# The expert pass of a two-block network: fixed order of experts, weights in a ring of slots, split products

## The reference, cut to what matters

```python
g_top = top_1(t @ rg_w + rg_b)                # 1 of 4 groups
e_top = top_2(t @ re_w[g] + re_b[g])          # 2 of its 4 experts
for e in range(16):
    hid = silu(t @ w_gate[e]) * (t @ w_up[e])             # 1024 -> 512
    out = out + combine[:, e:e+1] * (hid @ w_down[e])     # 512 -> 1024
return rms_norm_2(h + out, final_norm_g)
```

## Time and profile before

| | us |
|---|---|
| median of 3 runs | 2615.15 (2611.01 to 2625.91) |
| the profiled execution, its own time | 2606.21 |
| its span | 2604.4 |
| TensorE busy (PE), share of the span | 2364.2, 91% |
| VectorE busy (DVE), share | 1160.2, 45% |
| ScalarE busy (ACT), share | 587.6, 23% |
| GpSimd busy (POOL), share | 731.7, 28% |
| mean granted TensorE clock | 0.95 |

### The profile page before, as it was taken

How to read it: one execution, slowest core, us unless ns; L and a number is a source line. 1 busy time by engine, 2 the same in 40 slices (tenths; PEclk the granted TensorE clock), 3 DMA queues, 4 the chain that set the end, 5 groups by cost and what they waited for, 6 DMA issues and landing times.

```text
span 2604.4 us, 28182 instructions
## 1 busy us (share of the span) xinstructions
PE 2364.2 (91%) x10934; PEld 1736.5 (67%) x10934; DVE 1160.2 (45%) x1501; ACT 587.6 (23%) x851; POOL 731.7 (28%) x420
## 2 busy tenths in 40 slices
PE   6899988899999999898998999998996885999994
PEld 3576637688888888664556888886875673444442
DVE  2488963364444443336645646542228422111113
ACT  2311113311111111325633111122334120110111
POOL 2100002533333334434335444444430331000001
PEclk8999987899999999999998999998999986999997
DMA  8445241262122221210012333232320224888885
GB/s 267 158 161 162 97 162 41 73 227 65 58 63 64 64 65 57 71 41 9 1 31 79 95 96 97 89 115 67 97 81 1 80 57 142 309 315 324 315 321 186
DMA packets 242054, 312.67 MB, mean 120 GB/s; under 512 B 13499, under 2 KB 199468, under 8 KB 235828
## 3 DMA queue, kind: packets, MB, share of 16 engines
q1 hardware_dynamic: 230140, 275.23, 32.4%
q0 software_dynamic: 7040, 25.72, 2.6%
q10 hardware_dynamic: 4791, 10.58, 1.1%
HBM read 286.31 MB, written 25.19 MB: 120 GB/s over the span
## 4 chain that ended last, share of the span: by engine, by line
PE 78%; issue 8%; DVE 6%; POOL 4%; DMA 3%; ACT 1%; DVEq 0%; POOLq 0%; ACTq 0%
PE acc L475 49%; PE acc L2151 9%; PE pb L2166 4%; PE pb L1827 2%; PE pa L1779 2%; PE acc L1953 2%; PE pa L1967 2%; PE pb L1980 2%; DMA mod_raw<-in_w_mod 2%; POOL wlo L458 1%; PE acc L522 1%; POOL y L601 1%; DVE hid_hi L1321 1%; PE acc L536 1%; PE pa L629 1%
## 5 line engine op out<-in xcount | busy, mean ns | idle before, releaser
L458 POOL TENSOR_TENSOR wlo<-raw,whi 128x1024 fp32r<-128x1024 f32 x204 | 509.2, 2496 | 969.1 <-ACT whi L447 969.0
L475 PE MATMUL acc<-ah,whi 128*128 128x256 f32 (+1 forms) x1616 | 514.7, 367 | 58.6 <-DVE al L641 36.2
L475 PE MATMUL acc<-al,whi 128*128 128x256 f32 (+1 forms) x1616 | 506.7, 362 | 0.0
L475 PE MATMUL acc<-ah,wlo 128*128 128x256 f32 (+1 forms) x1616 | 505.8, 362 | 0.0
L447 ACT ACTIVATE whi<-raw 128x1024 fp32r<-128x1024 f32 x218 | 230.3, 1059 | 1057.6 <-PE acc L475 1038.8
L475 PEld LDWEIGHTS acc<-ah,whi 128*128 128x128 f32 x1616 | 306.6, 191 | 120.6 <-issue 42.4
L475 PEld LDWEIGHTS acc<-al,whi 128*128 128x128 f32 x1616 | 309.8, 192 | 47.0 <-issue 0.5
L475 PEld LDWEIGHTS acc<-ah,wlo 128*128 128x128 f32 x1616 | 308.9, 191 | 46.9
L1330 DVE SCALAR_TENSOR_TENSOR x<-acc,mod,x 128x256 f32<-128x256 f32 (+1 forms) x192 | 121.1, 658 | 262.1 <-PE acc L475 262.0
L475 PE MATMUL acc<-hid_hi,whi 128*128 128x512 f32 (+1 forms) x768 | 230.8, 355 | 0.7 <-DVE x L1330 0.2
L475 PE MATMUL acc<-hid_lo,whi 128*128 128x512 f32 (+1 forms) x768 | 229.6, 353 | 0.0
(11 more groups left out here) (310 smaller groups left out, 2487.9 us busy)
## 6 DMA issues: line engine op xcount, KB each, us to landing
raw<-in_w_ff SPq DMA_DIRECT2D x128, 512.0 KB, 3.9
mod_raw<-in_w_mod SPq DMA_DIRECT2D x96, 512.0 KB, 5.3
wg<-in_expert_w_gate SPq DMA_DIRECT2D x16, 2048.0 KB, 8.6
wu<-in_expert_w_up SPq DMA_DIRECT2D x16, 2048.0 KB, 8.7
wd<-in_expert_w_down SPq DMA_DIRECT2D x16, 2048.0 KB, 10.0
raw<-in_w_in SPq DMA_DIRECT2D x30, 512.0 KB, 3.9
raw<-in_conv_w_pw SPq DMA_DIRECT2D x24, 512.0 KB, 7.2
expert_rows_dram<-zero_rows POOLq DMA_DIRECT2D x1, 12288.0 KB, 38.2
```

What stands on the lines that cost most here:

```text
L458: e.eng.tensor_tensor(wlo[b][:, :], raw[e.n["g"] % RING][:, :], whi[b][:, :].bitcast(F32), ALU.subtract).then_inc(S["lo_ready"], 1)
L475: ins = e.eng.matmul(o, w, m, start=keys.index(key) == n, stop=len(keys) - 1 - keys[::-1].index(key) == n)
```

## The change

The 48 KB in which wg, wu and wd lay become a ring of 12 slots of 1,024 values a partition (4 gate, 4 up, 4 down), loaded in pairs of 1 MB. ScalarE writes the high part of a slot into one of five buffers; VectorE writes the low part over the slot itself. The ten slots of gate, up and the first two of down are split so and multiplied in three fp32r terms; the last two of down stay f32. The rows and half of the hidden values are split too. The down product of a block is done one pass late, after the next block's gate and up products.

The list of blocks now begins with every expert once, in order, and further blocks of experts with more than 128 rows come behind. So the first two blocks need no routing result: the loads of the first expert's 12 slots are issued before the last projection is done, and the code of blocks 0 and 1 stands ahead of the loop, which runs over the rest (`more`, 14 here). A counter `weights_used` numbers the slots as TensorE uses them; all waits of SyncE, ScalarE and VectorE for free space are values of it. `count_of(i, each, more)` is i x each + more for the pair i = (loop variable, offset). One semaphore per pair of slots tells that its load has landed (before: one each for wg, wu and wd). The old loops are taken out (their lines are left out below).

```diff
+E_SLOTS = 12
+SPLIT_DOWN = 2
+E_SPLITS = 8 + SPLIT_DOWN
+E_HIGHS = 5
...
-    wg = sb("wg", [P, KT, E_FF], at=ah_at)
-    wu = sb("wu", [P, KT, E_FF], at=ah_at + 16384)
-    wd = sb("wd", [P, 4, D], at=ah_at + 32768)
+    expert_pair = [sb(f"expert_pair{r}", [P, 2 * D], at=ah_at + 8192 * r) for r in range(E_SLOTS // 2)]
+    expert_in = [expert_pair[r // 2][:, r % 2 * D:r % 2 * D + D] for r in range(E_SLOTS)]
+    expert_lo = [sb(f"expert_lo{r}", [P, D], F32R, ah_at + 4096 * r) for r in range(E_SLOTS)]
+    expert_hi = [sb(f"expert_hi{b}", [P, D], F32R, e_at + 4096 * b) for b in range(E_HIGHS)]
...
-    xgt = sb("xgt", [P, KT, P], at=h_at + 20480)
+    xgt_hi = sb("xgt_hi", [P, KT, P], F32R, h_at + 20480)
+    xgt_lo = sb("xgt_lo", [P, KT, P], F32R, h_at + 43008)
...
+    hidT_hi = sb("hidT_hi", [P, 4, P], F32R, h_at + 28672)
+    hidT_lo = sb("hidT_lo", [P, 4, P], F32R, h_at + 47104)
...
+    def weights_done(i, s):
+        return s + 1 if i is FIRST else count_of(i, E_SLOTS, s - 3)
+    def split_number(i, s):
+        return s if i is FIRST else count_of(i, E_SPLITS, s - SPLIT_DOWN)
+    def high_buffer(i, s):
+        return expert_hi[(s if i is FIRST else 8 + s) % E_HIGHS]
+    def expert_load(e, ex, s):
+        if s < 8:
+            src = A["expert_w_gate_2" if s < 4 else "expert_w_up_2"][0, ex].rearrange("e (p k) n -> p (e k n)", k=KT)
+        else:
+            src = A["expert_w_down_2"][0, ex].rearrange("e (p k) n -> p (e k n)", k=4)
+        e.eng.dma_start(expert_pair[s // 2][:, :], src[:, s % 4 * D:s % 4 * D + 2 * D]
+                        ).then_inc(S[f"expert_in{s // 2}"], 16)
+    def expert_high(e, i, s, n):
+        e.eng.wait_ge(S[f"expert_in{s // 2}"], count_of(i, 16, 16 if s < 8 else 0))
+        if i is not FIRST or n >= E_HIGHS:
+            e.eng.wait_ge(S["weights_used"], weights_done(i, n - E_HIGHS))
+        e.eng.activation(high_buffer(i, n)[:, :], expert_in[s][:, :], ACT.Copy).then_inc(S["expert_hi"], 1)
+    def expert_low(e, i, s, n):
+        e.eng.wait_ge(S["expert_hi"], split_number(i, n) + 1)
+        e.eng.tensor_tensor(expert_lo[s][:, :], expert_in[s][:, :], high_buffer(i, n)[:, :].bitcast(F32), ALU.subtract
+                            ).then_inc(S["expert_lo"], 1)
...
+        sp.wait_ge(S["acc_ready"], U_TOTAL - KT)
+        for s in range(0, E_SLOTS, 2):
+            expert_load(e, slice(0, 1), s)
...
+        for s in range(0, 8, 2):
+            sp.wait_ge(S["weights_used"], s + 2)
+            expert_load(e, slice(1, 2), s)
         sp.wait_ge(S["meta_ready"], 1)
...
+        more = sp.value_load(meta[0:1, LIST:LIST + 1], min_val=N_EXP - 2, max_val=SLOTS_MAX - 2)
+        def expert_of(i):
+            return bass.ds(sp.value_load(meta[0:1, bass.ds(count_of(i, 1, 0), 1)], min_val=0, max_val=N_EXP - 1), 1)
+        def load_parts(i, parts):
+            ex = expert_of(i)
+            for s in parts:
+                sp.wait_ge(S["weights_used"], weights_done(next_to(i, -1 if s < 8 else 0), s + 1))
+                expert_load(e, ex, s)
+        with sp.Fori(0, more) as i:
+            load_parts((i, 2), range(0, 8, 2))
+            load_parts((i, 1), range(8, E_SLOTS, 2))
+        load_parts((more, 1), range(8, E_SLOTS, 2))
...
+        def rows_high(i):
+            act.wait_ge(S["xg_turned"], count_of(i, 1, 2))
+            act.activation(xgt_hi[:, :, :], pa[:, :].rearrange("p (k q) -> p k q", q=P), ACT.Copy
+                           ).then_inc(S["xgt_hi"], 1)
+        def silu(i):
+            act.wait_ge(S["weights_used"], weights_done(i, 3))
+            if i is not FIRST:
+                act.wait_ge(S["hidt_ready"], count_of(i, 1, 0))
+            act.activation(gate_s[:, :], acc[0][:, 0:E_FF], ACT.Silu).then_inc(S["silu_gate"], 1)
+        def out_half(i, last=3):
+            act.wait_ge(S["weights_used"], weights_done(next_to(i, 1), last))
+            act.wait_ge(S["yo_out"], count_of(i, 16, 16))
+            act.activation(yo[:, 0:512], pbk[:, 0:512], ACT.Copy).then_inc(S["yo_act"], 1)
+        def out_rows(i):
+            act.wait_ge(S["yo_act"], count_of(i, 1, 1))
+            act.wait_ge(S["yo_dve"], count_of(i, 1, 1))
+            act.dma_start(yo_d[bass.ds(count_of(i, P, 0), P), :], yo[:, :]).then_inc(S["yo_out"], 16)
+        def expert_first():
+            expert_high(e, FIRST, 0, 0)
+            rows_high(FIRST)
+            for s in range(1, 8):
+                expert_high(e, FIRST, s, s)
+            silu(FIRST)
+        def expert_pass(i, rows_out):
+            expert_high(e, i, 0, 0)
+            rows_high(i)
+            for s in range(1, 4):
+                expert_high(e, i, s, s)
+            if rows_out:
+                out_half(next_to(i, -2), 11)
+            for s in range(4, 6):
+                expert_high(e, i, s, s)
+            if rows_out:
+                out_rows(next_to(i, -2))
+            for s in range(6, 8):
+                expert_high(e, i, s, s)
+            silu(i)
+            for s in range(8, 8 + SPLIT_DOWN):
+                expert_high(e, i, s, s)
+        expert_first()
+        expert_pass((None, 1), False)
         act.wait_ge(S["meta_ready"], 1)
...
+        more = act.value_load(meta[0:1, LIST:LIST + 1], min_val=N_EXP - 2, max_val=SLOTS_MAX - 2)
+        with act.Fori(0, more) as i:
+            expert_pass((i, 2), True)
+        for n in range(SPLIT_DOWN):
+            expert_high(e, (more, 2), 8 + n, n)
+        out_half((more, 0), 11)
+        out_rows((more, 0))
+        out_half((more, 1))
+        out_rows((more, 1))
...
+        base, further = rt[:, 17, 0:16], rt[:, 17, 16:32]
+        e.step(TS(base, ramp[:, 0:16], float(P), 16.0 * P, ALU.mult, ALU.add))
+        e.step(TT(further, upto, nb, ALU.subtract))
+        e.step(TT(further, further, ramp[:, 0:16], ALU.subtract))
+        e.step(TS(further, further, float(P), -float(P), ALU.mult, ALU.add))
+        ranks = pbk[:, 512:576].rearrange("p (b n) -> p b n", b=4)
         where = rt[:, 18, 0:64].rearrange("p (b n) -> p b n", b=4)
-        e.step(TT(where, pbk[:, 512:576].rearrange("p (b n) -> p b n", b=4),
-                  base.unsqueeze(1).to_broadcast([P, 4, 16]), ALU.add))
+        beyond = rt[:, 22, 0:64].rearrange("p (b n) -> p b n", b=4)
+        e.step(TS(beyond, ranks, float(P), None, ALU.is_ge))
+        e.step(TT(beyond, beyond, further.unsqueeze(1).to_broadcast([P, 4, 16]), ALU.mult))
+        e.step(TT(where, ranks, base.unsqueeze(1).to_broadcast([P, 4, 16]), ALU.add))
+        e.step(TT(where, where, beyond, ALU.add))
...
+        def rows_low(i):
+            dve.wait_ge(S["xgt_hi"], count_of(i, 1, 1))
+            TT(xgt_lo[:, :, :], pa[:, :].rearrange("p (k q) -> p k q", q=P), xgt_hi[:, :, :].bitcast(F32), ALU.subtract
+               ).then_inc(S["xgt_ready"], 1)
+        def hidden(i):
+            dve.wait_ge(S["silu_gate"], count_of(i, 1, 1))
+            dve.wait_ge(S["weights_used"], weights_done(i, 7))
+            TT(hidt[:, :], gate_s[:, :], acc[0][:, 512:1024], ALU.mult).then_inc(S["hidt_ready"], 1)
+        def hidden_turned(i):
+            dve.wait_ge(S["hid_turned"], count_of(i, 1, 1))
+            turned = acc[1][:, 0:E_FF].rearrange("p (k q) -> p k q", q=P)
+            if SPLIT_DOWN < 4:
+                dve.tensor_copy(hidT[:, SPLIT_DOWN:, :], turned[:, SPLIT_DOWN:, :])
+            dve.tensor_copy(hidT_hi[:, 0:SPLIT_DOWN, :], turned[:, 0:SPLIT_DOWN, :]).then_inc(S["hidT_high"], 1)
+            dve.wait_ge(S["hidT_high"], count_of(i, 1, 1))
+            TT(hidT_lo[:, 0:SPLIT_DOWN, :], turned[:, 0:SPLIT_DOWN, :], hidT_hi[:, 0:SPLIT_DOWN, :].bitcast(F32),
+               ALU.subtract).then_inc(S["hidT_ready"], 1)
+        def out_half(i, last=3):
+            dve.wait_ge(S["weights_used"], weights_done(next_to(i, 1), last))
+            dve.wait_ge(S["yo_out"], count_of(i, 16, 16))
+            dve.tensor_copy(yo[:, 512:1024], pbk[:, 512:1024]).then_inc(S["yo_dve"], 1)
+        def expert_first():
+            expert_low(e, FIRST, 0, 0)
+            rows_low(FIRST)
+            for s in range(1, 8):
+                expert_low(e, FIRST, s, s)
+            hidden(FIRST)
+        def expert_pass(i, rows_out):
+            expert_low(e, i, 0, 0)
+            rows_low(i)
+            for s in range(1, 4):
+                expert_low(e, i, s, s)
+            if rows_out:
+                out_half(next_to(i, -2), 11)
+            hidden_turned(next_to(i, -1))
+            for s in range(4, 8 + SPLIT_DOWN):
+                expert_low(e, i, s, s)
+            hidden(i)
+        expert_first()
+        expert_pass((None, 1), False)
         dve.wait_ge(S["meta_ready"], 1)
...
+        more = dve.value_load(meta[0:1, LIST:LIST + 1], min_val=N_EXP - 2, max_val=SLOTS_MAX - 2)
+        with dve.Fori(0, more) as i:
+            expert_pass((i, 2), True)
+        for n in range(SPLIT_DOWN):
+            expert_low(e, (more, 2), 8 + n, n)
+        out_half((more, 0), 11)
+        hidden_turned((more, 1))
+        out_half((more, 1))
```

(115 more changed lines are left out.)

49 lines of the change are left out of this document (3 added, 46 removed).

## The result

| | before | changed |
|---|---|---|
| median, us | 2617.06 (4 runs) | 2553.28 (4 runs, 2548.43 to 2561.81) |
| profiled execution, us | 2606.21 | 2548.4 |
| its span, us | 2604.4 | 2546.7 |
| PE / DVE / ACT / POOL busy, share of the span | 91 / 45 / 23 / 28% | 91 / 53 / 29 / 29% |

The ratio is 0.976 (95% interval 0.972 to 0.980). A later comparison of the same two kernels gave 2554.45 against 2610.58, ratio 0.980 (0.977 to 0.982). The forecast was 2553.

What follows compares the result with a forecast made beforehand. TensorE's own instructions bound the pass: 1.2 + 19.0 + 15 x 18.93 + 7.8 = 312.0 us against 374.1, a gain of 62.1; from the median 2615.15 that gives 2553 us, 8-in-10 range 2538 to 2590.

Steps and rivals of the forecast that it cites:

- The period: TensorE's time per expert block: 60 three-term matmuls, four f32 matmuls and transposes, 18.93 us in place of 23.18.
- Hand-offs covered: Forming and copying hidden rows in each pass lies beside other TensorE work; uncovered it would cost 2.3 us again.
- VectorE and ScalarE: Added splitting work per expert pass, 16.1 us on VectorE and 14.1 on ScalarE, fits beside TensorE's 18.93 and costs nothing.
- Rivals 2 and 3: Expert pass: VectorE's low parts too late, 2578 us, chance 0.06; at 2.5 us per part, slower, 2722 us, chance 0.04.
- Rival 4: No change: TensorE's clock falls in the expert pass, 8.5 us at half clock eating the gain, 2617 us; chance 0.03.
- Transfers: Expert pass needs 388 GB/s; bounds were 20.2 us by busy share or 17.8 to 18.3 by fast stretches, the latter taken.
- The step trusted least: Expert stretch: transfers keep 388 GB/s for 280 us, though no stretch of the trace was longer than 8 us.
- rival 1: Transfers become the bound of the expert pass, 20.2 us each by busy share, 19 us more, 2572 us; chance 0.18.
- Routing: Ahead of the expert pass: more small and 64-column steps on the chain to the positions, +1.2 us.
- Start of block 0: First expert block: high and low rows made in series where one copy stood before, 1.1 us more.
- The scatter: Ahead of the expert pass: early loads might free the scatter of one or two us, left out of the sum.
- The exit: After the last pass: the last block's hidden copies and down product, 7.8 us, loads having about 14 us before use.

Runs made afterwards that it cites:

- e4: Changed kernel with every product in f32 and no high or low parts, ring and late down product kept: 2587.07 us, 0.990 of the kernel before.
- e5: Changed kernel with the down product in its own block's pass, behind the turn of the hidden rows: 2570.8 us, 0.983 of the kernel before.
- e2: Changed kernel with all four down slots in three terms and six high buffers: 2541.57 us, 0.973 of the kernel before.
- e7: Changed kernel with one more unused load of 1 MB in each looped pass: 2569.91 us, 0.981 of the kernel before.
- e8: Changed kernel with 0.5 MB more loaded in each looped pass: 2551.03 us, 0.978 of the kernel before.
- e6: Changed kernel with the first expert's 6 MB of weights issued behind the routing result: 2565.82 us, 0.981 of the kernel before.
- e1: Changed kernel with the last block's down weights loaded earlier, into the first four slots: 2544.22 us, 0.974 of the kernel before.
- e3: Changed kernel with e1's early last down weights and e2's fully split down product together: 2534.25 us, 0.971 of the kernel before.

## Why the prediction was right, and where not

The time was 2553.0 against 2553.28. The mechanism was right; that the number agrees so closely is luck, as the terms were less exact than that. By the profiled executions the gain is 57.8 us where 62.1 was given; the median of the second comparison gives 56.1, that of the first 63.8.

- **Bound.** TensorE's own instructions, before and after: right, shown by the chain and by TensorE busy 243.44 of 243.44 us.
- **The period.** 18.93 given, 18.73 measured. The three-term matmul was put at 0.2286 and takes 0.232 in the pass (11.14 / 48), 0.2 us a pass too low; the twelve transposes were put at 1.77 and take 1.36, 0.4 too high (eight in 0.89, four in 0.47; the 0.59 for four came from a row that stands behind a wait). Over 15 passes the sum was 2.7 us too high (283.95 against 281.2).
- **Hand-offs covered.** Right: e4 puts their price before at 1.2 us a pass, e5 at 2.0 if they were opened again now. Even the small waits for low parts that the prediction allowed for didn't come.
- **VectorE and ScalarE.** 16.1 and 14.1 us given, 15.3 and 12.4 measured in the window, which counts overlapping records once; the operations' means add up to 16.1 and 12.8. The low parts took 1.22, as given. The hidden copies 0.41 each against 0.42. ScalarE reloads no table in the loop, 1.28 us a pass less. Rivals 2 and 3 are out: the longest of the 160 low parts took 1.232 us, and at 96% (e2) VectorE still isn't waited for. Rival 4 is out too, with a granted clock of 1.00 over the 243 us.
- **Transfers.** The choice between the bounds was right and too careful: 402 to 412 taken, 422 sustained (e7). The step trusted least, 388 GB/s for 280 us, held with 390 over 243. The other bound, 20.2 us from the busy share, fails, and rival 1 with it: e8 moves 421 GB/s in passes of 18.73. By the Trainium skill, HBM Reference, section Specifications (TRN2), the share of 358 GB/s doesn't bind here; its 425 for a core that streams alone agrees with the 422 measured.
- **Routing.** +1.2 given; from the last step of the choice (L1663) to the end of the positions (L1696) 10.76 us before, 11.94 after: +1.18.
- **Start of block 0.** +1.1 given, +0.97 measured (3.35 us from turn to first product, now 4.32). Block 0: 17.9 given, 17.2 measured.
- **The scatter.** Left out as one or two us; 5.58 us of wait became 1.45, a gain of 4.1. e6 shows the cause: row numbers scattered while weight loads are in flight land later, the more the more bytes are in flight. How the loads hold them up isn't shown. The row stood in the trace of before, with a 2 MB load in flight, and I had read it as an issue time.
- **The exit.** The step of the prediction that failed: "the last block's hidden copies and down product ... 7.8 us", and with it "each has about 14 us before its slot is needed". It is 15.3 us. The down slots are one pass late, so the last block's first pair can be issued only when block 14's is used up, and there are no up slots left to cover it: 4.88 us of load, two high and two low parts, the hidden copies queued behind them on VectorE, then half clock. e1 takes 5.5 us of it away.

Measured less given, the errors were -2.7 (passes), -0.7 and -0.1 (block 0), +7.5 (exit), -4.1 (scatter). They cancel to within a microsecond. What is left between 62.1 and 57.8 is that everything ahead of the routing's end came about 5 us later in this execution; as that stage moves by up to 20 us among kernels with the same code there, it is put down to noise.

## What to carry to other kernels

When a ring with a delayed stage is costed by its steady pass, cost its last pass by itself: the loads that the delay postpones have no work left beside them, and slots that have run out of users can take them. Where a pass is bound by TensorE's f32 products, three fp32r terms (0.696 us here against 0.859, 19% less) pay only if the splitting engines and the transfers keep up; add up the work of each per pass beside TensorE's before anything else. Small scattered DMAs on the critical chain land sooner with no bulk load in flight: issue the bulk loads early enough to have landed.

## What the runs showed of the hardware that I had not expected

- The DMA share reads 0.95 at 333 GB/s (e4), 1.00 at 390, 1.01 at 407 and 422. It is full before the rate is: it can't be turned into a floor of time.
- 421 to 422 GB/s of mixed traffic (weights read, one gather and one store per pass) held over 210 us on one core.
- After the last of eight scatters of row numbers GpSimd waited 1.45, 5.58 or 11.81 us for them to land, with none, 2 MB or 6 MB of loads in flight.
- 1.8 us of idle TensorE ahead of the last product was followed by half clock for about 3.4 us of it (e1), and 2.0 us likewise (e3), while the kernel before kept full clock through two gaps of 0.34 us in each pass. But e4 kept full clock behind a gap of 1.96 us, and e5, with a gap of 1.6 us in every pass, fell to half clock behind one of its 16. The length of the gap alone doesn't tell; what does isn't shown.
- Three-term fp32r matmuls of 512 columns came 0.227 us apart in an earlier projection and 0.232 in this pass. What makes the difference is open.
